# Latent attention stage: another order of DVE's and ACT's steps around the query's low halves, the key's reciprocal and the first scores

## The reference

```python
def mla_queries(h, wq_a, q_a_norm, wq_b, q_norm):
    cq = rmsnorm(h @ wq_a, q_a_norm)
    q = (cq @ wq_b).reshape(B, S, MLA_HEADS, QK_DIM)
    return rmsnorm(q, q_norm)

def mla_keys_values(h, wkv_a, kv_a_norm, wkv_b, k_norm):
    kv_a = h @ wkv_a
    ckv, k_pe = kv_a[..., :KV_LORA], kv_a[..., KV_LORA:]
    kv = (rmsnorm(ckv, kv_a_norm) @ wkv_b).reshape(B, S, MLA_HEADS, QK_NOPE + V_DIM)
    k_nope, v = kv[..., :QK_NOPE], kv[..., QK_NOPE:]
    k = rmsnorm(jnp.concatenate([k_nope, k_pe], axis=-1), k_norm)
    return k, v
```

## Time and profile before

| | |
|---|---|
| Time, median of 3 runs | 991.48 us (991.28 to 992.29) |
| Span of the profiled execution, first to last instruction | 987.1 us |
| TensorE busy | 943.5 us, 96% of the span |
| DVE busy | 706.0 us, 72% |
| ACT busy | 538.3 us, 55% |
| POOL busy | 309.0 us, 31% |
| Mean granted TensorE clock | 0.975 of full speed |
| DMA | 195.60 MB, mean 198 GB/s |

### The profile page before, as it was taken

The page is one execution under the profiler, slowest core; times in us unless marked ns, Lnnn a source line. Parts: engine busy times, 40 slices in busy tenths (PEclk is TensorE's granted clock), DMA queues, the critical chain, the costliest instruction groups (busy, mean ns, idle before and its releaser), DMA issues.

```text
span 987.1 us, 19548 instructions
## 1 busy us (share of the span) xinstructions
PE 943.5 (96%) x6882; PEld 871.3 (88%) x6882; DVE 706.0 (72%) x1132; ACT 538.3 (55%) x921; POOL 309.0 (31%) x272
## 2 busy tenths in 40 slices
PE   5988989999999999999979999999999999999996
PEld 5877556799999999988969999999999879899996
DVE  4997778678988777897886688555555773475664
ACT  3464655565765444654634666654444761674645
POOL 1942122237997111120051288640110000330012
PEclk9898999999999999999979999999999998999999
DMA  9856175168878777788615676555555332255521
GB/s 351 292 182 239 42 226 171 47 218 309 309 271 275 284 267 279 244 324 283 225 61 171 234 256 214 186 176 190 171 192 182 130 95 98 86 172 173 169 87 43
DMA packets 57052, 195.60 MB, mean 198 GB/s; under 512 B 6303, under 2 KB 9791, under 8 KB 56736
## 3 DMA queue, kind: packets, MB, share of 16 engines
q1 hardware_dynamic: 55312, 192.36, 56.7%
q0 software_dynamic: 1680, 2.44, 1.1%
HBM read 192.65 MB, written 1.07 MB: 196 GB/s over the span
## 4 chain that ended last, share of the span: by engine, by line
PE 85%; DVE 9%; ACT 2%; issue 2%; DMA 1%; POOL 0%; SPq 0%; DVEq 0%; ACTq 0%
PE bank L526 24%; PE bank L527 24%; PE bank L528 24%; DVE w_lo L1576 2%; PE bank L791 1%; PE bank L925 1%; PE bank L951 1%; PE bank L624 1%; PE bank L782 1%; DMA x<-x_in 1%; PE bank L824 1%; PE bank L633 1%; PE bank L879 1%; DVE ada_raw L1678 1%; DVE ada_raw L1591 1%
## 5 line engine op out<-in xcount | busy, mean ns | idle before, releaser
L1576 DVE TENSOR_TENSOR w_lo<-raw,w_hi 128x1024 fp32r<-128x1024 f32 (+1 forms) x261 | 340.0, 1304 | 108.0 <-ACT w_hi L1146 106.1
L1146 ACT ACTIVATE w_hi<-raw 128x1024 fp32r<-128x1024 f32 (+1 forms) x261 | 272.4, 1044 | 174.4 <-PE bank L528 166.4
L526 PE MATMUL bank<-act_hi,w_hi 128*128 128x258 f32 (+1 forms) x872 | 251.5, 288 | 0.0
L527 PE MATMUL bank<-act_lo,w_hi 128*128 128x258 f32 (+1 forms) x872 | 248.0, 284 | 0.0
L528 PE MATMUL bank<-act_hi,w_lo 128*128 128x258 f32 (+1 forms) x872 | 247.5, 284 | 0.0
L526 PEld LDWEIGHTS bank<-act_hi,w_hi 128*128 128x128 f32 x872 | 166.1, 190 | 3.3 <-issue 2.8
L527 PEld LDWEIGHTS bank<-act_lo,w_hi 128*128 128x128 f32 x872 | 166.1, 190 | 1.0 <-issue 1.0
L528 PEld LDWEIGHTS bank<-act_hi,w_lo 128*128 128x128 f32 x872 | 166.1, 190 | 0.0
L528 PE MATMUL bank<-hid_hi,w_lo 128*128 128x256 f32 x512 | 143.4, 280 | 0.0
L526 PE MATMUL bank<-hid_hi,w_hi 128*128 128x256 f32 x512 | 142.8, 279 | 0.0
L527 PE MATMUL bank<-hid_lo,w_hi 128*128 128x256 f32 x512 | 142.8, 279 | 0.0
(11 more groups left out here) (349 smaller groups left out, 1812.7 us busy)
## 6 DMA issues: line engine op xcount, KB each, us to landing
raw<-weights SPq DMA_DIRECT2D x247, 512.0 KB, 3.6
ada_raw<-ada SPq DMA_DIRECT2D x88, 512.0 KB, 4.8
raw<-weights SPq DMA_DIRECT2D x14, 384.0 KB, 4.3
ada_more<-ada SPq DMA_DIRECT2D x8, 512.0 KB, 6.4
bias<-bias_by_distance SPq DMA_DIRECT2D x1, 2048.0 KB, 9.1
x<-x_in SPq DMA_DIRECT2D x1, 1024.0 KB, 7.3
ctx<-ctx_in SPq DMA_DIRECT2D x1, 1024.0 KB, 9.5
out<-result SPq DMA_DIRECT2D x4, 256.0 KB, 2.7
```

Of the source, the lines that this page charges most:

```text
L526: pe.matmul(dst, w[0], a[0], start=start, stop=False)
L527: pe.matmul(dst, w[0], a[1], start=False, stop=False)
L1146: act.activation(w_hi[:, slot, 0:width_of(c)], raw[:, slot, 0:width_of(c)], ACT.Copy).then_inc(weight_hi, 1)
L1576: dve.tensor_tensor(w_lo[:, slot, 0:w], raw[:, slot, 0:w], w_hi[:, slot, 0:w].bitcast(fp32), ALU.subtract).then_inc(weight_lo, 1)
```

## The change

**Query stage.** PE's `query_sums(i)` for the eight heads waits for the high half (`q_high`), which ACT makes right after the squares that are summed, and no longer for the bank to be free, which DVE's low half reports. The wait for all twelve banks now stands before the last of the five rotations, the one that writes bank 3. On DVE `query_low(4)` goes ahead of `convert(14)`, and `query_low(6)` and `query_low(7)` go ahead of `modulate(3)` and `convert(16)`; `convert(17)` goes into the key loop. ACT makes the high halves of the latent before `convert(16)`, not after it. Two of the four low halves of the latent go from POOL to DVE, between `convert(14)` and `convert(15)`.

**Key loop.** DVE gets `convert(17)` at head 2, `modulate(5)` at head 3 and `modulate(6)` at head 6. ACT's copy `qr_hi` comes after head 6, not after head 7 and a conversion.

**Before the scores.** ACT takes the key's root first, then the query's, and then one exponential of a 128 x 1 column whose result nobody uses, so that the function table is loaded here. DVE inverts the key's root right after the key loop, makes the low half `k_rstd_lo` before `qr_lo`, and does `convert(19)`, `modulate(7)`, `convert(20)`, `modulate(8)` and `convert(21)` after them. `convert(21)` and `modulate(8)` stood behind the first logits before; now both are ahead of them.

```diff
@@ PE
             def query_sums(i):
-                pe.wait_ge(evacuated, group0["q_b"] + i + 1)
+                if i >= 4:
+                    pe.wait_ge(q_high, i - 3)
+                else:
+                    pe.wait_ge(evacuated, group0["q_b"] + i + 1)
...
+            pe.wait_ge(evacuated, group0["q_b"] + 12)
             pe.matmul(bank[3][:, 0:S], rot, kpe[:, CTX:SC], start=True, stop=True).then_inc(rotated, 1)
@@ ACT
+                if i == 4:
+                    for k in range(4):
+                        split(split0["ckv"] + k, ckv_hi[:, k // 2, (k % 2) * S:(k % 2 + 1) * S])
                 convert(chunk0["q_b"] + i + 4)
...
-                if i == 4:
-                    for k in range(4):
-                        split(split0["ckv"] + k, ckv_hi[:, k // 2, (k % 2) * S:(k % 2 + 1) * S])
...
-            act.wait_ge(qr_turned, 1)
-            act.activation(qr_hi[:], qr, ACT.Copy).then_inc(qr_high, 1)
+                if h == 6:
+                    act.wait_ge(qr_turned, 1)
+                    act.activation(qr_hi[:], qr, ACT.Copy).then_inc(qr_high, 1)
+            root(std[0:H, :], bank[4][0:H, :], QK, k_sums, H, k_std)
             act.wait_ge(q_sum_added, 1)
...
-            root(std[0:H, :], bank[4][0:H, :], QK, k_sums, H, k_std)
+            act.activation(small[:, 95:96], eps[:], ACT.Exp)
@@ DVE
-            convert(14)
             query_low(4)
+            convert(14)
+            for k in (2, 3):
+                dve.wait_ge(split_hi, split0["ckv"] + k + 1)
+                dve.tensor_tensor(ckv_lo[:, 1, (k - 2) * S:(k - 1) * S], tile_f32[:, (split0["ckv"] + k) % 4, :],
+                                  ckv_hi[:, 1, (k - 2) * S:(k - 1) * S].bitcast(fp32), ALU.subtract).then_inc(split_lo, 1)
             convert(15)
             query_low(5)
-            modulate(3)
-            convert(16)
             query_low(6)
             query_low(7)
+            modulate(3)
+            convert(16)
             modulate(4)
-            convert(17)
...
+                if h == 2:
+                    convert(17)
                 if h == 3:
                     convert(18)
+                    modulate(5)
+                if h == 6:
+                    modulate(6)
...
-            modulate(5)
-            convert(19)
+            dve.wait_ge(k_std, 1)
+            dve.reciprocal(rstd[0:H, :], std[0:H, :]).then_inc(k_inverse, 1)
             dve.wait_ge(q_std, 1)
...
-            dve.wait_ge(qr_high, 1)
-            dve.tensor_tensor(qr_lo[:], qr, qr_hi[:].bitcast(fp32), ALU.subtract).then_inc(q_ready, 1)
-            dve.wait_ge(k_std, 1)
-            dve.reciprocal(rstd[0:H, :], std[0:H, :]).then_inc(k_inverse, 1)
-            modulate(6)
             dve.wait_ge(k_rstd_high, 1)
             dve.tensor_tensor(k_rstd_lo[:], rstd[0:H, :], k_rstd_hi[:].bitcast(fp32), ALU.subtract).then_inc(k_rstd, 1)
+            dve.wait_ge(qr_high, 1)
+            dve.tensor_tensor(qr_lo[:], qr, qr_hi[:].bitcast(fp32), ALU.subtract).then_inc(q_ready, 1)
+            convert(19)
             modulate(7)
             convert(20)
+            modulate(8)
+            convert(21)
...
-                if u < 2 * H:
-                    if u == 0:
-                        convert(21)
+                if 1 <= u < 2 * H:
                     modulate(8 + u)
@@ POOL
-            for k in range(4):
-                tok = slice((k % 2) * S, (k % 2 + 1) * S)
-                split(split0["ckv"] + k, ckv_hi[:, k // 2, tok], ckv_lo[:, k // 2, tok])
+            for k in range(2):
+                tok = slice(k * S, (k + 1) * S)
+                split(split0["ckv"] + k, ckv_hi[:, 0, tok], ckv_lo[:, 0, tok])
```

More of the change, by code:

```diff
@@ L1739, in _ @@
                     query_low(3)
+            query_low(4)
             convert(14)
-            query_low(4)
+            for k in (2, 3):
+                dve.wait_ge(split_hi, split0["ckv"] + k + 1)
+                dve.tensor_tensor(ckv_lo[:, 1, (k - 2) * S:(k - 1) * S], tile_f32[:, (split0["ckv"] + k) % 4, :],
+                                  ckv_hi[:, 1, (k - 2) * S:(k - 1) * S].bitcast(fp32), ALU.subtract).then_inc(split_lo, 1)
             convert(15)
             query_low(5)
+            query_low(6)
+            query_low(7)
             modulate(3)
             convert(16)
-            query_low(6)
-            query_low(7)
             modulate(4)
-            convert(17)
             dve.wait_ge(q_sums_read, 1)
@@ L1791, in _ @@
             then(dve.tensor_scalar(q_scale[:, 1], q_scale[:, 0], -1.0, None, ALU.mult))
+            dve.wait_ge(k_rstd_high, 1)
+            dve.tensor_tensor(k_rstd_lo[:], rstd[0:H, :], k_rstd_hi[:].bitcast(fp32), ALU.subtract).then_inc(k_rstd, 1)
             dve.wait_ge(qr_high, 1)
             dve.tensor_tensor(qr_lo[:], qr, qr_hi[:].bitcast(fp32), ALU.subtract).then_inc(q_ready, 1)
-            dve.wait_ge(k_std, 1)
-            dve.reciprocal(rstd[0:H, :], std[0:H, :]).then_inc(k_inverse, 1)
-            modulate(6)
-            dve.wait_ge(k_rstd_high, 1)
-            dve.tensor_tensor(k_rstd_lo[:], rstd[0:H, :], k_rstd_hi[:].bitcast(fp32), ALU.subtract).then_inc(k_rstd, 1)
+            convert(19)
             modulate(7)
             convert(20)
+            modulate(8)
+            convert(21)
             def normalise(a, u, dst, sinks=False, rows=64):
```

## The result

The changed kernel took 982.66 us, median of 4 runs (980.0 to 984.12), beside 991.88 us for the kernel before in the same comparison (4 runs, 991.28 to 994.74). The ratio is 0.9901 with a 95% interval of 0.9878 to 0.9923. A second comparison, on another chip, gave 982.18 us (6 runs, 979.8 to 983.98) beside 992.67 us (11 runs), ratio 0.9905 (0.988 to 0.993). So the gain is 0.95 to 1.0%, and 983.1 us was forecast.

The account below looks back on a forecast made before the run. TensorE was taken as the bound, busy 943.5 of 987.1 us. Gains 5.9 + 0.2 + 1.65 + 0.6 = 8.35 us gave 978.75, plus 4.4 to the median: 983.1 us; 8-in-10 range 980.9 to 986.6.

Parts of the forecast that it names:

- Query stage: Sum 8 to the keys: idle time and half clock go, keys start at 92.15; 6.3 us with the first key head.
- the take-off from the sum: Query stage: 5.9 us taken, not 6.3, because the long half clock was partly chance of one execution.
- Key loop: Key heads: DVE's added work fits with slack 0.2, costing nothing; 0.4 us of wait if one conversion takes 1.75.
- The key's reciprocal: Value projection: earlier reciprocal gains 0.2 us of the 1.3 wait; TensorE's idle there shrinks to 0.7, third value tile 0.45 late.
- The rival with the drain: Early table load: a drain makes ACT 1.4 us later; gain 6.95 or 5.3, 984.5 to 986.2 us; chance 0.06.
- Clock of the value projection: Value tiles 5 to 7: with 0.7 us idle the clock does not fall; gain 1.65 us, bounds 0 and 1.65.
- First scores: After TensorE's first score: first logits 1.4 us later, at +3.0, yet first transpose at +5.65 before 6.25; gain 0.6 us.
- From the sum to the median: Whole kernel: 4.4 us, by which the median exceeds the profiled span, added to 978.75 to give 983.1 us.
- a later stage is shifted as a whole: Sign in the profile: stages from 190 us on move earlier as a whole; otherwise the prediction is wrong.

Follow-up runs that it names:

- the rest alone: Changed kernel with the query stage as before and without its move of chunk 17's conversion; 987.54 us (10 runs), ratio 0.9968 against the kernel before.
- old DVE order: Changed kernel with DVE's query-stage order as before, the sums' new wait and DVE's two latent low halves kept; query stage 5.76 us, for 3.75 in the changed kernel.
- POOL makes four: Changed kernel with all four low halves of the latent made by POOL, none by DVE; query stage 4.08 us, for 3.75 in the changed kernel.
- query part: Kernel before with only the change's query stage and chunk 17's conversion in the key loop; 984.25 us (4 runs), ratio 0.9932 against the kernel before.
- filled wait: Kernel before with 22 more matmuls, whose result nobody reads, ahead of sum 10; query stage 7.19 us, for 9.90 before; total 992.12 us in one run.
- old wait: Changed kernel with the sums waiting again for the low halves and no separate wait at the last rotation; query stage 6.71 us, for 3.75 in the changed kernel.

## Why the prediction was right

**Query stage: right, the take-off from the sum was wrong.** The working gave 3.75 from sum 8 to the keys (88.4 to 92.15), and 3.75 was measured; the keys stand at 93.33 and not at 92.2 only because the stage began at 89.58, 1.2 us later. What was taken off, 0.4 for a half clock that may have been long by chance, was not there: 6.15 and the 0.08 in the keys are 6.23, where 6.3 was worked out and 5.9 taken. The one other trace with the old stage whole, the rest alone, has 9.58 + 21.81 = 31.39 us for the two stages, beside 30.92 before, so it does vary, and there to the other side. The old DVE order confirms that both halves of the edit are needed, POOL makes four that the latent's two low halves do what the prediction said of them: "what lets the keys start at that time", by 0.33 us. (The steps that the prediction gives DVE behind 90.4 add up to 93.9, not to its 94.1; nothing hangs on it.)

**Key loop: right.** No wait of TensorE but the first 0.90. `kn_lo` started 6.86 us after sum 8, forecast 6.8 (95.2 less 88.4).

**The key's reciprocal: right in size.** The wait for `k_rstd_lo` is 0.58 (forecast 0.7), its cause the fourth evacuation ahead of `k_rstd_hi`, as stated: the order exchanged, the wait was gone. From the first value tile to the fifth 9.38 us passed (123.65 less 114.27) for 9.72 before, so 0.34 won where 0.2 was forecast. ACT's timeline of the changed kernel answers to the earlier trace rows, TensorE's to the earlier trace rows:

```profile
115.46 1.28 ACT L1308 ACT_TABLE_LOAD   x1
116.76 0.20 ACT L1308 ACTIVATE small<-eps 128x1 f32<-128x1 f32 x1
116.86 1.11 ACT L1165 ACTIVATE v_mla<-bank 128x512 f32<-128x512 f32 x2
```

```profile
117.50 0.50 PE L526 MATMUL bank<-w_hi,om_hi 128*128 128x512 f32 x1 [0.15 <-ACT v_mla L1165]
...
122.54 0.49 PE L747 MATMUL bank<-k_rstd_hi,heads 8*128 8x512 f32 x1 [0.58 <-DVE k_rstd_lo L1807]
...
123.65 0.49 PE L526 MATMUL bank<-w_hi,om_hi 128*128 128x512 f32 x1
...
127.95 0.40 PE L526 MATMUL bank<-kn_hi,act_hi 128*128 128x512 f32 x1
```

For the third value tile 0.45 late was forecast; the profile lists 0.15 of wait, and the kernel without the load shows that the price is 0.41. The rival with the drain fell: the little exponential starts 1.30 us after the load began, and the activation before had ended at 115.45. The rule of the Trainium skill (ScalarE: Activation LUTs, What ACT_TABLE_LOAD costs) agrees on the load itself, about 1.28, but its drain of about 1.38 us is not seen at any of the loads shown here, and the measurement decides.

**Clock of the value projection: right.** The last three tiles took 127.95 - 123.65 = 4.30 us for 5.85, 1.55 of the 1.65 forecast. This is more than one lucky run: behind the wait of 1.32 us the clock fell in 3 kernels of 3 (before, query part, filled wait), behind 0.58 to 0.59 in none of 8, and without the wait in none of 3.

**First scores: right in size.** 0.72 us won, 0.6 forecast. The first transpose came 5.52 after the first score (5.65 forecast), the first logits at 2.92 (3.0 forecast), with DVE waiting for ACT's half of chunk 21. DVE's timeline of the changed kernel, which answers to the earlier trace rows, and TensorE's:

```profile
129.73 1.22 DVE L1582 TENSOR_TENSOR w_lo<-raw,w_hi 128x1024 fp32r<-128x1024 f32 x1 [1.42 <-ACT w_hi L1150]
130.87 0.68 DVE L1833 CUSTOM_DVE_ANT_0 scaled<-bank,sq 128x512 f32<-128x512 f32 x1
```

```profile
133.47 0.66 PE L786 MATMUL bank<-const,p_mla 128*128 128x128 f32 x4 [0.22 <-DVE p_mla L1824]
...
136.08 0.66 PE L786 MATMUL bank<-const,p_mla 128*128 128x128 f32 x4 [0.59 <-DVE p_mla L1824]
```

**From the sum to the median: the right figure with a wrong name.** The prediction added 4.4 us "by which the median exceeds this span". Around the span there are only 1.8 us (984.12 against 982.3). The other 2.6 were the profiled execution of before, faster than its median. That is worked out and not measured: no time is on record for that execution. Since only a difference is carried to the median, it did no harm: 991.48 - 8.84 = 982.64, and 982.66 was measured. That these agree so closely is luck, as is the hit to 0.4 us. The medians fell by 9.2 us in one comparison and by 10.5 in the other, each uncertain by more than 2, so the times cannot tell the forecast 8.35 from 8.84. The stages can.

**That a later stage is shifted as a whole: half wrong.** The profiled spans differ by 4.8 us only, 987.1 against 982.3. TensorE's landmarks of the changed kernel stand 7.7 us earlier at 144 us (8.84 less the 1.2 by which the query stage began later), 8.3 at 513, 8.0 at 830, and 4.8 at the end. Stretches of the kernel before and then of the changed kernel (length; busy time of PE, PEld, DVE, ACT, POOL; clock; DMA):

```profile
810.00:870.00 60.00, 57.66 (x451) 53.71 (x450) 29.07 (x45) 29.91 (x51) 12.40 (x15) 0.94 0.31 104
```

```profile
810.00:870.00 60.00, 57.67 (x425) 54.17 (x425) 29.48 (x47) 29.07 (x50) 15.71 (x17) 0.89 0.34 111
```

TensorE is busy for the same time, but with a mean clock of 0.89 for 0.94: at half speed for some 6 us longer (0.05 x 2 x 60), which costs 3 us. Nothing of the change lies there. The mean was 0.89 to 0.91 in every trace of a kernel with the query part or one half of it, and 0.94 in that of the rest alone, so a link with the shift is not ruled out. But it was 0.91 in the filled wait too, whose latent layer ends no earlier than before. And the timed runs speak against a lasting loss: the median of their mean clocks is 0.974 in 11 runs of the kernel before and 0.979 in 6 of the changed one. That is about 10 us less at half speed (0.005 x 2 x 985), just what the two stages of the latent layer save by the stretches of 2 us (6.8 and 3.4). So it may be the trace of the kernel before that was fast here by chance; that stays open.

## What to carry to other kernels

Let a consumer wait for the first thing that is enough for it, and ask at once which later step waits for the old thing: here the wait moved to the last rotation and would have kept 2.0 of the 6.15 us, had DVE's order not been changed with it. Price a wait of TensorE with what the clock does behind it: filled with idle matmuls, the same wait cost 2.7 us less. And test each part of a change that wins: two parts of this one, the early table load and the conversion ahead of the first logits, lost 0.41 and 0.87 us under the cover of the others.

## What the runs showed of the hardware

**The clock does not follow the length of the last wait.** It fell behind 0.94 us of idle time between one-column sums (old wait, 0.58 from 92 to 94 us), and it did not fall behind 1.73 us after rotations of 256 columns (old DVE order, whose query stage was 5.76, just the wait longer). Behind the 0.89 to 0.90 us ahead of head 2 in the key loop, nearly as long as the 0.94, it fell in none of the 14 traces. After 1.63 us ahead of the first transposes it fell in two kernels (query part, filled wait) and not in the kernel before. What the chip weighs is not settled by these runs.

**DVE and POOL hold each other up.** With four subtractions on POOL (5.75 us, till 93.03), DVE's modulation and conversion at 90.68 and 92.36 took 1.75 each. In the changed kernel POOL was through with its two at 91.92, and the same two of DVE, at 91.94 and 93.14, took 1.28 and 1.22. The two conversions before them took 1.22 each beside POOL as well, and there POOL's two took 4.05 us, 2.0 each. In the old DVE order, again with two on POOL, these took 2.11, and it was DVE's own two subtractions of the latent beside them that took 1.51 for 0.76. That the overlap is the cause is read from these traces; no run tests it by itself. The Trainium skill (GPSIMD Engine Reference, Specifications) says that POOL's interfaces to SBUF are shared with VectorE, with contention where a DVE instruction reads two inputs from there. The trace agrees, and it shows which side pays: either one.
